# Forgetting attention in a three-layer transformer kernel: normalised queries and keys turned by VectorE and moved within SBUF

## What is computed

```python
proj = h @ w_in
q, k, v, g, z_f = jnp.split(proj, [D, 2 * D, 3 * D, 4 * D], axis=-1)
q = rmsnorm(q.reshape(B, T, H, Dh), q_norm_g).transpose(0, 2, 1, 3)
k = rmsnorm(k.reshape(B, T, H, Dh), k_norm_g).transpose(0, 2, 1, 3)
log_f = jax.nn.log_sigmoid(z_f + b_f)
c = jnp.cumsum(log_f, axis=1).transpose(0, 2, 1)
s = jnp.einsum('bhqd,bhkd->bhqk', qi, k) * scale      # scale = 1/sqrt(64)
s = s + cqi[..., None] - c[:, :, None, :]              # causal mask follows
p = jax.nn.softmax(s, axis=-1)
o = jnp.einsum('bhqk,bhkd->bhqd', p, v)
o = o.transpose(1, 0, 3, 2, 4).reshape(B, T, D) * jax.nn.sigmoid(g)
return o @ w_out
```

## Time and profile before

| what | value |
|---|---|
| median of 3 runs | 1580.67 us (1580.09 to 1581.17) |
| the profiled execution's own time | 1580.04 us |
| its span, first to last instruction | 1578.2 us |
| VectorE busy | 1130.0 us (72%) |
| ScalarE busy | 825.0 us (52%) |
| mean granted TensorE clock | 0.999 of full speed |
| HBM and SBUF traffic of the DMA engines | 337.09 MB, mean 214 GB/s |

### The profile page before, as it was taken

How to read it: one execution, slowest core, us unless ns; L and a number is a source line. 1 busy time by engine, 2 the same in 40 slices (tenths; PEclk the granted TensorE clock), 3 DMA queues, 4 the chain that set the end, 5 groups by cost and what they waited for, 6 DMA issues and landing times.

```text
span 1578.2 us, 22308 instructions
## 1 busy us (share of the span) xinstructions
PE 1563.0 (99%) x8273; PEld 1294.6 (82%) x8273; DVE 1130.0 (72%) x1271; ACT 825.0 (52%) x1007; POOL 67.1 (4%) x101
## 2 busy tenths in 40 slices
PE   8999999999999999999999999999999999999998
PEld 6888888888888888887888888888887988878886
DVE  6565668868776877776867877787787567775654
ACT  6465564654445544465655444554447666574443
POOL 2000100000000000000000000000000000000000
PEclk9999999999999999999999999999999999999999
DMA  8766653359887688845345988668884444456662
GB/s 281 223 206 215 228 200 123 129 173 299 278 264 260 209 276 281 280 165 182 109 159 186 301 265 276 236 217 271 274 306 153 171 161 149 145 173 214 210 208 87
DMA packets 242385, 337.09 MB, mean 214 GB/s; under 512 B 14217, under 2 KB 180322, under 8 KB 242320
## 3 DMA queue, kind: packets, MB, share of 16 engines
q1 hardware_dynamic: 196320, 281.05, 53.9%
q0 software_dynamic: 11232, 39.33, 6.8%
q10 hardware_dynamic: 34768, 15.83, 4.0%
HBM read 319.38 MB, written 1.05 MB: 203 GB/s over the span
## 4 chain that ended last, share of the span: by engine, by line
PE 94%; DVE 3%; ACT 2%; DMA 1%; issue 0%; SPq 0%; DVEq 0%; ACTq 0%
PE ps L602 28%; PE ps L604 28%; PE ps L603 28%; PE ps L654 3%; PE ps L662 2%; PE ps L611 1%; DVE w_lo L1928 1%; ACT w_hi L1370 1%; DMA raw<-ffn_w_in_dram 1%; DVE arena L1963 0%; PE ps L877 0%; PE ps L1037 0%; PE ps L1063 0%; PE ps L1187 0%; ACT arena L1418 0%
## 5 line engine op out<-in xcount | busy, mean ns | idle before, releaser
L1928 DVE TENSOR_TENSOR w_lo<-raw,w_hi 128x2048 fp32r<-128x2048 f32 x264 | 601.7, 2288 | 198.0 <-ACT w_hi L1370 196.9
L1370 ACT CAST w_hi<-raw 128x2048 fp32r<-128x2048 f32 x264 | 502.1, 1911 | 322.1 <-PE ps L604 290.1
L602 PE MATMUL ps<-w_hi,actT_hi 128*128 128x512 f32 x1392 | 546.5, 393 | 1.1 <-ACT arena L1687 0.7
L604 PE MATMUL ps<-w_hi,actT_lo 128*128 128x512 f32 x1392 | 542.1, 389 | 0.0
L603 PE MATMUL ps<-w_lo,actT_hi 128*128 128x512 f32 x1392 | 541.8, 389 | 0.0
L602 PEld LDWEIGHTS ps<-w_hi,actT_hi 128*128 128x128 f32 x1392 | 261.3, 188 | 57.9 <-issue 3.3
L604 PEld LDWEIGHTS ps<-w_hi,actT_lo 128*128 128x128 f32 x1392 | 261.3, 188 | 54.6
L603 PEld LDWEIGHTS ps<-w_lo,actT_hi 128*128 128x128 f32 x1392 | 261.4, 188 | 53.3
L602 PE MATMUL ps<-w_hi,hT_hi 128*128 128x512 f32 x480 | 187.4, 390 | 0.0
L604 PE MATMUL ps<-w_hi,hT_lo 128*128 128x512 f32 x480 | 186.9, 389 | 0.0
L603 PE MATMUL ps<-w_lo,hT_hi 128*128 128x512 f32 x480 | 186.8, 389 | 0.0
(11 more groups left out here) (304 smaller groups left out, 1301.3 us busy)
## 6 DMA issues: line engine op xcount, KB each, us to landing
raw<-ffn_w_in_dram SPq DMA_DIRECT2D x172, 512.0 KB, 4.9
raw<-ffn_w_out_dram SPq DMA_DIRECT2D x88, 512.0 KB, 4.6
arena<-w_ada_dram POOLq DMA_DIRECT2D x72, 512.0 KB, 5.3
raw<-ffn_w_gate_dram SPq DMA_DIRECT2D x44, 512.0 KB, 4.0
raw<-ffn_w_up_dram SPq DMA_DIRECT2D x44, 512.0 KB, 5.0
raw<-ffn_w_down_dram SPq DMA_DIRECT2D x44, 512.0 KB, 4.4
raw<-w_in_dram SPq DMA_DIRECT2D x40, 512.0 KB, 4.5
raw<-hg_w_in_dram SPq DMA_DIRECT2D x32, 512.0 KB, 4.7
```

What stands on the lines that cost most here:

```text
L602: nc.tensor.matmul(to, hi, whi, start=start, stop=False, skip_group_check=True)
L604: return nc.tensor.matmul(to, lo, whi, start=False, stop=stop, skip_group_check=True)
L1370: nc.scalar.copy(w_hi[:, s, :], raw[:, s, :]).then_inc(hi_ready[s], 1)
L1928: nc.vector.tensor_tensor(w_lo[:, s, :], raw[:, s, :], w_hi[:, s, :].bitcast(F32), ALU.subtract)\
```

## The change

The 16 TensorE transposes of each half go. `normed` now writes its result into a region `fx_rows`, reading every fourth value of a head so that channel 4n + q lands in group q. One VectorE transpose (`turn` on VectorE, 128x2048) turns all 32x32 blocks of a half into `fx_blocks`, over the place of `fx_qk`. ScalarE issues four transfers within SBUF for each half (`move`), each from 32 partitions to all 128 of `fx_columns`, 256 KB each, 1 MB for a half. `queries` and `keys` read `fx_columns` in place of PSUM, once for each token tile with 512 values a partition. `squared(1)` now waits for `keys(0)`, since `fx_columns` lies over `fx_sq`. On ScalarE `move(0)` stands ahead of `queries(0)`, and `move(1)` between the fourth and the fifth exponential of `exps(1)`. On VectorE `turn(0)` stands behind `forget_gates`, and `turn(1)` ahead of `keys(1)`. On TensorE `weigh(0)` no longer stands behind a `turn(1)`, and the wait for `fx_qT_ready` ahead of `unit(5, 1)` goes.

```diff
@@ -279,6 +279,10 @@
...
+        def fx_turned_columns(chunks, t):
+            return fx_columns.rearrange("p a (t m i) -> p t m a i", t=TILES, m=KD)[:, t, chunks]
         def hg_kept(c, t):
@@ -302,6 +306,9 @@
...
         fx_v, fx_g, fx_sq = region(4096, TILES, D), region(6144, TILES, D), region(6144, TILES, D)
+        fx_rows = region(6144, 4, TILES, COLS // 2)
+        fx_blocks = [region(2048 * half, 4, COLS) for half in range(2)]
+        fx_columns = region(6144, 4, COLS)
         fx_oT, fx_y = region(0, KD, T), region(2048, 4, 4, P)
@@ -1006,24 +1013,12 @@
...
-                def turn(half, banks):
-
-                    for t in range(TILES):
-                        pe.wait_ge(fx_normed, 2 * half + t + 1)
-                    for n, bank in enumerate(banks):
-                        if bank == 5:
-                            pe.wait_ge(fx_negc_ready, 3)
-                        for kk in range(2):
-                            for t in range(TILES):
-                                at = COLS * (1 - n // 2) + (2 * (n % 2) + kk) * P
-                                last = nc.tensor.transpose(ps[:, bank, kk * T + t * P:kk * T + (t + 1) * P],
-                                                           fx_qk[half][:, t, at:at + P], ident)
-                        last.then_inc(fx_turned, 1)
-
                 def score(g):
...
                     first = (4, 1)[g % 2]
-                    if g == 1:
+                    if g == 0:
+                        pe.wait_ge(fx_negc_ready, 3)
+                    elif g == 1:
                         pe.wait_ge(kept0, st.kept + 4)
@@ -1054,8 +1049,7 @@
...
                     if g == 1:
-                        pe.wait_ge(fx_qT_ready, 4)
-                        pe.wait_ge(fx_kT_ready, 4)
+                        pe.wait_ge(fx_max, 2)
                     s = fx_s[g % 2]
@@ -1087,7 +1081,6 @@
...
                 spread_gates()
-                turn(0, (6, 7, 4, 5))
                 chunk(st, 1, 1)
@@ -1095,11 +1088,8 @@
...
                 unit(5, 0)
-                pe.wait_ge(fx_max, 2)
+                weigh(0)
                 pe.wait_ge(kept1, st.kept + 5)
-                turn(1, (1, 2, 3, 7))
-                weigh(0)
-                pe.wait_ge(fx_qT_ready, 4)
                 unit(5, 1)
@@ -1673,6 +1663,7 @@
...
                                 act.wait_ge(fx_mean, 2)
+                                act.wait_ge(fx_kT_ready, 2)
                         nc.scalar.activation(fx_sq[:, t, :], fx_qk[half][:, t, :], ACT.Square).then_inc(fx_squared, 1)
@@ -1680,17 +1671,24 @@
...
-                def queries(half, banks):
-                    for n, bank in enumerate(banks):
-                        b = 2 * half + n
-                        act.wait_ge(fx_turned, 4 * half + 2 + n + 1)
-                        nc.scalar.activation(fx_qT[:, 2 * b:2 * b + 2, :], ps[:, bank, :].rearrange("p (k t) -> p k t", k=2),
-                                             ACT.Copy, scale=q_g8_col).then_inc(fx_qT_ready, 1)
+                def move(half):
+                    act.wait_ge(fx_turned, half + 1)
+                    for q in range(4):
+                        nc.scalar.dma_start(fx_columns[:, q, :], fx_blocks[half][32 * q:32 * q + 32, :, :]).then_inc(fx_moved, 16)
+                def queries(half):
+                    act.wait_ge(fx_moved, 64 * (half + 1))
+                    for t in range(TILES):
+                        to = fx_qT[:, 4 * half:4 * half + 4, t * P:(t + 1) * P].rearrange("p m (a i) -> p m a i", a=4)
+                        nc.scalar.activation(to, fx_turned_columns(slice(0, 4), t), ACT.Copy, scale=q_g8_col).then_inc(fx_qT_ready, 1)
...
                     for i in range(8):
+                        if g == 1 and i == 4:
+                            move(1)
                         qb, hh = i // 4, i % 4
@@ -1714,7 +1712,8 @@
...
                 keep(2)
-                queries(0, (4, 5))
+                move(0)
+                queries(0)
                 weights(4)
@@ -1726,10 +1725,11 @@
...
                 keep(5)
-                queries(1, (3, 7))
+                queries(1)
                 weights(7)
...
                 exps(2)
+                act.wait_ge(fx_kT_ready, 4)
                 gate(6, 0)
@@ -2325,10 +2325,17 @@
...
                     for t in range(TILES):
-                        qk = fx_qk[half][:, t, :].rearrange("p (g n) -> p g n", n=FOX_D)
+                        qk = fx_qk[half][:, t, :].rearrange("p (g n q) -> p q g n", q=4, n=16)
                         at = 32 * half + 16 * t
-                        nc.vector.tensor_tensor(qk, qk, f_rstd[:, at:at + 16].unsqueeze(2).to_broadcast([P, 16, FOX_D]),
-                                                ALU.mult).then_inc(fx_normed, 1)
+                        rstd = f_rstd[:, at:at + 16].unsqueeze(1).unsqueeze(3).to_broadcast([P, 4, 16, 16])
+                        step.mark(nc.vector.tensor_tensor(fx_rows[:, :, t, :].rearrange("p q (g n) -> p q g n", n=16), qk, rstd,
+                                                          ALU.mult))
+                def turn(half):
+                    step.wait()
+                    nc.vector.transpose(fx_blocks[half].rearrange("p q n -> p (q n)"), fx_rows.rearrange("p q t n -> p (q t n)"))\
+                        .then_inc(fx_turned, 1)
@@ -2349,12 +2356,11 @@
...
-                def keys(half, banks):
-                    for n, bank in enumerate(banks):
-                        b = 2 * half + n
-                        dve.wait_ge(fx_turned, 4 * half + n + 1)
-                        nc.vector.tensor_scalar(fx_kT[:, 2 * b:2 * b + 2, :], ps[:, bank, :].rearrange("p (k t) -> p k t", k=2),
-                                                k_g_col, None, ALU.mult).then_inc(fx_kT_ready, 1)
+                def keys(half):
+                    dve.wait_ge(fx_moved, 64 * (half + 1))
+                    for t in range(TILES):
+                        to = fx_kT[:, 4 * half:4 * half + 4, t * P:(t + 1) * P].rearrange("p m (a i) -> p m a i", a=4)
+                        nc.vector.tensor_scalar(to, fx_turned_columns(slice(4, 8), t), k_g_col, None, ALU.mult).then_inc(fx_kT_ready, 1)
@@ -2419,9 +2425,10 @@
...
                 forget_gates()
+                turn(0)
                 keep(2)
                 spread_gates()
-                keys(0, (6, 7))
+                keys(0)
                 weights(4)
@@ -2431,7 +2438,8 @@
...
                 keep(4)
-                keys(1, (1, 2))
+                turn(1)
+                keys(1)
                 inverse_sums(0)
```

More of the change, by code:

```diff
@@ L368, in build @@
             "fx_z", "fx_sp", "fx_lf", "fx_c", "fx_spread", "fx_negc_hi", "fx_negc_ready"))
-        fx_squared, fx_mean, fx_std, fx_normed, fx_turned, fx_qT_ready, fx_kT_ready = (sem(n) for n in (
-            "fx_squared", "fx_mean", "fx_std", "fx_normed", "fx_turned", "fx_qT_ready", "fx_kT_ready"))
+        fx_squared, fx_mean, fx_std, fx_turned, fx_moved, fx_qT_ready, fx_kT_ready = (sem(n) for n in (
+            "fx_squared", "fx_mean", "fx_std", "fx_turned", "fx_moved", "fx_qT_ready", "fx_kT_ready"))
         fx_even, fx_scored, fx_max, fx_exp, fx_pT, fx_pT_act, fx_pT_dve, fx_pv, fx_gate, fx_o, fx_product = (sem(n) for n in (
```

## The result

The changed kernel takes 1586.5 us, the kernel before 1580.67 (medians of seven runs each); the ratio is 1.0040 with a 95% interval of 1.0029 to 1.0051. The forecast was 1582.4 with a range up to 1586.0, so the measured time lies 0.5 us above the range. The sign of the forecast (+1.7 us) was right, its size was less than a third of the +5.8 us measured.

The account below looks back on a forecast made before the run. TensorE, busy 99% of the span, bounds the kernel; from K on VectorE sets the pace. The 5.0 us gained turn into 6.8 us of waits: 1580.67 + 1.7 = 1582.4 us, range 1577.6 to 1586.0.

Parts of the forecast that it names:

- What goes from TensorE: Transposes of both halves and a wait behind `weigh(0)` leave TensorE: 2.41 + 1.84 + 0.74 = 5.0 us gained.
- VectorE's operations: On VectorE, `normed` costs 1.3 us more a half, the transpose takes 2.3, `keys` 0.9 in place of 1.41.
- The move: Four transfers within SBUF for each half: 4.75 to 6.0 us from transpose end to last landing, outer ends 4.2 and 7.5.
- M0: Half 0's time from the end of the transpose to the last landing, where no load runs: 5.4 us.
- M1: Half 1's time from the end of the transpose to the last landing, beside loads: 6.2 us.
- the fixed part: The part of a move's time besides the data's own: 2.1 − 0.26 = 1.84 us.
- K: Time at which VectorE begins `keep(3)`, from which VectorE sets the pace: 745.2, before 745.51.
- rival B: At `keys(1)` and through `weights(4)`: moves are slow, kernel slower by over 0.2%, 1586.4; 0.30 together with rival C.
- rival C: TensorE's clock falls in the new waits, 2 us of work lost, 1584.4; 0.30 together with rival B.
- The waits themselves: TensorE waits 2.8 us for `w_lo` ahead of `unit(5, 0)` and 4 us ahead of `weigh(1)`.
- a wait there: On TensorE at `score(2)`: a wait standing there would show the prediction wrong.
- Half 0: Both `weights(4)` slots are there when `unit(4, 0)` needs them, at 745.0 and 747.8, so it costs TensorE nothing.

Follow-up runs that it names:

- e8: Changed kernel with ScalarE's and VectorE's lists reordered so both moves travel while their engines work, and contiguous `normed` reads: 1575.75 us.
- e2: Changed kernel with each of the four transfers moving only the first half of each piece, 128 KB in place of 256 KB: 1581.54 us.
- e3: Changed kernel with 26 extra TensorE transposes of a constant in the wait ahead of `weigh(1)`: 1585.62 us.
- e4: Changed kernel with the products of `normed` reading their head's values contiguously, gains permuted alike: 1583.38 us.
- e10: Changed kernel with the transfers of partitions 32 and 96 issued on GpSimd's queue, the others staying on ScalarE's: 1587.42 us.
- e5: Changed kernel with half 1 turned by TensorE again, only half 0 going by the new way: 1581.88 us.
- e6: Changed kernel with half 0 turned by TensorE again, only half 1 going by the new way: 1584.41 us.
- e9: Changed kernel with the four transfers of a move issued in partition order 0, 64, 32, 96: 1585.48 us.
- e1: Changed kernel with each transfer reading 512 values from all 128 partitions in place of 2048 from 32: 1581.77 us.

## Why the prediction was wrong in size

**What goes from TensorE: right.** 5.0 us were counted; e8, where nothing new is waited for, gains 5.0 us at `weigh(1)` and 4.5 in the medians.

**VectorE's operations: right, but for 0.2 us.** Transpose 2.27 and 2.30 us (2.3 taken), `keys` 0.88 (0.9), `normed` 1.5 us more for a half (1.3 taken, 1.5 the upper end).

**The move: the term that was mis-sized.** M0 was taken as 5.4 and M1 as 6.2 us; both measured 7.2. The data's rate had been set between 250 GB/s, the average of this queue over the span, and 359 GB/s, a stretch of loads from HBM. The second does not read SBUF, and the first comes from transfers of a quarter of the size; e2 puts the rate at about 200 GB/s, and the two stretches of the move above had 157 and 225. By the share that the earlier trace rows uses, the 2.10 MB that this queue moves more in the changed kernel come to about 210 GB/s (an estimate, from rounded shares). The four issues, taken as 2.53 us, took 4.08. For half 1 the fixed part was taken from the most favourable place: the 2.1 us of the earlier trace rows are from 850:856, while the same transfers in 863:870 of the kernel before, beside more loads, took 4.2 to 4.6 us to land. By the prediction's own sum M0 and M1 of 7.2 are +1.8 at K and +1.0 at `keys(1)`. K, shifted, was 747.30 in place of 745.2 (+2.1, of which 1.8 are the move and 0.2 the strided reads), and from K to the end of `turned_p(1)` 787.88 − 750.29 = 37.59 us passed in place of 36.85 (+0.7: 1.0 more for the move, 0.3 less for VectorE's own work, 30.36 in place of 30.65). So `weigh(1)` came 784.99 − 782.1 = 2.9 us later than forecast. This is rival B, given with C 0.30.

**The clock: rival C, on top of B.** The prediction counted C as another case, not as an addition: in its sum the clock costs nothing. In both waits of TensorE the clock fell: 0.67 in 766:770 and 0.73 in 786:790. `unit(5, 0)` took 774.63 − 767.39 = 7.2 us in place of 5.6, which the wait at `weigh(1)` swallowed. Behind `weigh(1)` nothing swallows it: 1.3 us there and 0.2 in `unit(6, 0)` (796.64 − 790.73 = 5.9 in place of 5.7). The sum is 1.7 + 2.9 + 1.5 = 6.1 us at the end of the stage. The profiled spans differ by 1584.6 − 1578.2 = 6.4, 0.3 of it behind the stage; the medians by 5.8. The waits themselves had been forecast at the right two places, as 2.8 and 4 us; 3.55 and 2.89 were measured, because the slow `unit(5, 0)` had moved 1.6 us from the second wait into work. One more miss is hidden in this: in e3, e4 and e10, where `unit(5, 0)` ran at full clock, 1.8, 1.7 and 1.2 us of waiting stand at `score(2)`, for `keep_result(0)`. The prediction named a wait there as a sign of being wrong; it had put all of it at `weigh(1)`.

**Not foreseen:** `turn_p(0)` waited 0.78 us for `exps(0)`, which came late with `weights(4)`; the wait for `w_lo` behind it covers this.

**Half 0** cost TensorE nothing up to `unit(4, 0)`, as said (0.18 us of wait at 748.21), and its price appeared later, through K. e5 and e6 give the shares that the sum had not separated: 1.7 and 4.2 us.

## What to carry to other kernels

Work taken off the bounding engine is a gain only if the work that takes its place has somewhere to wait: put the issue of a transfer and its consumer as far apart in the lists as the transfer is long, with the weights of the next product between them. Price a transfer by a measured one of its own size and its own partitions, not by the queue's average, and price a new wait of the matrix engine with its clock afterwards.

## What the runs showed of the hardware

- A transfer within SBUF from 32 partitions to 128, 256 KB each and four in a row, runs at about 200 GB/s and takes 7.2 us from the first issue to the last landing, 7.2 to 8.1 where loads travel beside it; the same bytes read from 128 partitions, each piece into its own partition, take 4.4 us at up to 387 GB/s, and 6.0 beside loads. The issues on ScalarE's queue stretch with it, 4.08 against 2.49 us for four.
- Reading float32 from SBUF with a step of four values costs VectorE 0.73 us more for 1024 values, with no PSUM in play (3.85 against 2.36 us for two).
- After a wait of TensorE of 2 us or more in this stage the granted clock mostly fell to its lower level (0.67 and 0.73 over 4 us in the change), and not by the length of the wait alone. Ahead of `unit(5, 0)` it fell after 2.06 us in e5, 2.27 in e2, 3.55 in the change and 3.56 in e9, and stayed at 1.00 after 2.06 in e1 and 3.56 in e3 and e10. What decides between the two stays open. The stretch of e3 behind that wait:

```profile
764.00:768.00 4.00, 3.46 (x15) 2.90 (x16) 4.00 (x4) 2.75 (x9) 0.00 (x0) 1.00 0.61 195
```
